# Head squares, gate scan, token sums and factors of a hybrid decoder layer in another order

## The reference

```python
xn = rmsnorm(x, norm_gain)
gb, gc, hc, zc, q, k, v, o, zm, ig, fg = split(xn @ w_in)        # nine of width 512, two of width 4
y_conv = gb * short_conv(gc * hc, conv_buf, conv_w) * silu(zc)   # 3 taps along the tokens
# mLSTM, 4 heads of 128, chunks of 128 tokens, one after another:
b = cumsum(log_sigmoid(fg)); log_d = causal(b[:, None] - b[None, :] + ig[None, :])
m_t = maximum(b + m_prev, max(log_d)); d = exp(log_d - m_t); inter = exp(b + m_prev - m_t)
s = (q @ k.T) * d
num = s @ v + inter * (q @ c_prev); den = sum(s) + inter * (q @ n_prev)
h = num / maximum(abs(den), exp(-m_t))
c_new = decay * c_prev + (w_last * k).T @ v                      # n_new likewise
h = h * rsqrt(mean(h * h) + EPS) * mh_norm_gain
y_m = h * sigmoid(o) * silu(zm)
out = rmsnorm(x + concat(y_conv, y_m) @ w_out, final_norm_gain)
```

## Time and profile before

| | |
|---|---|
| Median of 3 runs | 1103.79 us (1103.05 to 1104.08) |
| Profiled execution | 1105.74 us, its span 1103.7 us |
| TensorE matmul busy | 1027.2 us (93%) |
| TensorE weight load busy | 776.4 us (70%), beside the matmuls |
| DVE busy | 657.3 us (60%) |
| ACT busy | 423.4 us (38%) |
| POOL busy | 440.8 us (40%) |
| DMA | 180.86 MB, mean 164 GB/s |
| Chain that ended last | PE 61%, DVE 22%, ACT 5%, POOL 4%, issue 3%, DMA 3% |

### The profile page before, as it was taken

How to read it: one execution, slowest core, us unless ns; L and a number is a source line. 1 busy time by engine, 2 the same in 40 slices (tenths; PEclk the granted TensorE clock), 3 DMA queues, 4 the chain that set the end, 5 groups by cost and what they waited for, 6 DMA issues and landing times.

```text
span 1103.7 us, 22725 instructions
## 1 busy us (share of the span) xinstructions
PE 1027.2 (93%) x9052; PEld 776.4 (70%) x9052; DVE 657.3 (60%) x1156; ACT 423.4 (38%) x868; POOL 440.8 (40%) x477
## 2 busy tenths in 40 slices
PE   3799799999889988999999999999999999999995
PEld 2555545455478777999889899989889999444442
DVE  6786756664667776556775546567755544434343
ACT  6555443423334343334543443436343432211111
POOL 5211355445454484623542341427042330542422
PEclk9999899999889999999999999999999999999998
DMA  9686642924561256591605272943253659465651
GB/s 246 175 190 138 160 111 63 236 66 143 198 207 53 84 165 215 162 322 62 223 21 189 93 248 65 314 143 124 68 181 106 220 140 344 140 216 210 232 207 76
DMA packets 192077, 180.86 MB, mean 164 GB/s; under 512 B 44600, under 2 KB 152260, under 8 KB 191972
## 3 DMA queue, kind: packets, MB, share of 16 engines
q1 hardware_dynamic: 160880, 142.76, 41.8%
q0 software_dynamic: 7600, 25.03, 6.2%
q10 hardware_dynamic: 23492, 11.63, 3.6%
HBM read 120.48 MB, written 50.19 MB: 155 GB/s over the span
## 4 chain that ended last, share of the span: by engine, by line
PE 61%; DVE 22%; ACT 5%; POOL 4%; issue 3%; DMA 3%; SPq 1%; DVEq 0%; ACTq 0%; POOLq 0%
PE bank L1337 10%; PE bank L1339 10%; PE bank L1338 10%; PE bank L1562 4%; PE bank L1563 4%; PE bank L1561 4%; DVE xs L207 3%; DVE Wl L207 2%; DVE yc L207 2%; DVE gatebuf L207 2%; PE bank L1138 1%; PE bank L1140 1%; PE bank L1139 1%; PE bank L1494 1%; PE bank L1495 1%
## 5 line engine op out<-in xcount | busy, mean ns | idle before, releaser
L1337 PE MATMUL bank<-xTh,Wh 128*128 128x256 f16 x768 | 211.6, 275 | 12.8 <-ACT bank L207 8.1
L1338 PE MATMUL bank<-xTl,Wh 128*128 128x256 f16 x768 | 211.4, 275 | 0.0
L1339 PE MATMUL bank<-xTh,Wl 128*128 128x256 f16 x768 | 211.4, 275 | 0.0
L1138 PE MATMUL bank<-xTh,Wh 128*128 128x512 f16 (+2 forms) x440 | 122.8, 313 | 3.2 <-ACT tom L207 1.0
L1139 PE MATMUL bank<-xTl,Wh 128*128 128x512 f16 (+2 forms) x440 | 123.1, 312 | 0.0
L1140 PE MATMUL bank<-xTh,Wl 128*128 128x512 f16 (+2 forms) x440 | 123.1, 312 | 0.0
L1337 PEld LDWEIGHTS bank<-xTh,Wh 128*128 128x128 f16 x768 | 75.9, 99 | 25.8 <-ACT bank L207 6.9
L1338 PEld LDWEIGHTS bank<-xTl,Wh 128*128 128x128 f16 x768 | 75.9, 99 | 10.9 <-issue 0.7
L1339 PEld LDWEIGHTS bank<-xTh,Wl 128*128 128x128 f16 x768 | 75.9, 99 | 9.5
L1337 PE MATMUL bank<-xTh,xs 128*128 128x256 f16 x288 | 78.8, 274 | 2.0 <-DVE xs L207 2.0
L1339 PE MATMUL bank<-xTh,xs 128*128 128x256 f16 x288 | 78.9, 274 | 0.0
(11 more groups left out here) (529 smaller groups left out, 2857.1 us busy)
## 6 DMA issues: line engine op xcount, KB each, us to landing
xTh<-x_ops SPq DMA_DIRECT2D x12, 1280.0 KB, 8.9
xTl<-x_ops SPq DMA_DIRECT2D x12, 1280.0 KB, 12.2
wst<-in_w_in SPq DMA_DIRECT2D x25, 512.0 KB, 5.0
xs<-in_x_prompt SPq DMA_DIRECT2D x22, 512.0 KB, 4.0
y_ops<-ysumst POOLq DMA_DIRECT2D x16, 512.0 KB, 3.2
xTh<-x_ops SPq DMA_DIRECT2D x12, 512.0 KB, 5.0
xTl<-x_ops SPq DMA_DIRECT2D x12, 512.0 KB, 5.7
out<-xs POOLq DMA_DIRECT2D x11, 512.0 KB, 2.9
```

The source lines that it names most:

```text
L1138: mm(out, wh[:, k, :], xh, start=(k == 0), stop=False)
L1337: mm(out, wh[:, k, :], xh, start=(first and k == 0), stop=False, skip_group_check=not first)
L1338: mm(out, wh[:, k, :], xl, start=False, stop=False, skip_group_check=not first)
L1339: last = mm(out, wl[:, k, :], xh, start=False, stop=(k == KT // 2 - 1), skip_group_check=not first)
```

## The change

Normalisation of heads: all four squares stand behind ACT's seed of the first pair of the next block. `sel` is gone: its readers take the columns straight from `cols`, and a new semaphore `parts_ready` covers the exponents' operand. `den` comes in four instructions that read PSUM and `cols`, not five. `mhg` is scaled once at the start; the factor moves from the products `G` and `Gm` (and from `to`, `tom`) to `heads_out` and its sample counterpart. `factors` goes behind DVE's seed of the first pair.

Queues: gate scans of blocks 1 and 2 from GB to ZC, turns to O; x parts later on ACT and DVE (after `evacuate` and `at_end`); token sums spread in another way on POOL, ACT and DVE; for head 1 the weight splits in the order 0, 1 | 2, 3 (sums of pair 0) | 4 (V) | 5, 6, and SP loads ZC and O ahead of GB; `G` directly behind ZM's drain, with the mixed tile's products between. The diff, cut to its core (the indentation of the functions is taken off), first the constants:

```diff
-X_SQUARE = [{V: 6, Q: 7, GC: 8, HC: 9, ZC: 10, O: 11}, {K: 12, V: 13, Q: 14, HC: 15}, {K: 16}]
-X_PARTS = [{V: 5, Q: 6, GC: 7, HC: 8, ZC: 9, O: 10}, {K: 11, V: 12, Q: 13, HC: 14}, {K: 15, V: 16}]
+X_SQUARE = [{V: 6, Q: 7, GC: 8, HC: 9, ZC: 10, O: 11}, {K: 12, V: 13, Q: 14, O: 15}, {K: 16}]
+X_PARTS = [{V: 5, Q: 6, GC: 7, HC: 8, ZC: 9, O: 10}, {K: 11, V: 12, Q: 13, O: 14}, {K: 15, V: 16}]
...
-SCAN_AT = [O, GB, GB]
-TURN_AT = [ZM, ZC, ZC]
+SCAN_AT = [O, ZC, ZC]
+TURN_AT = [ZM, O, O]
...
-S_TAKE = [{}, {ZC: 0, ZM: 1}, {V: 2, HC: 3, ZM: 4}, {K: 5, Q: 6, HC: 7}]
-S_LOW = [{}, {ZC: 0, ZM: 1}, {V: 2, HC: 3, ZM: 4}, {K: 5, Q: 6, GB: 7}]
-S_STORE = [{}, {O: 0}, {K: 1, Q: 2, GB: 3}, {K: 4, V: 5, GC: 6, ZC: 7}]
+S_TAKE = [{}, {GC: 0, HC: 1}, {V: 2, GC: 3, ZC: 4, ZM: 5}, {Q: 6, HC: 7}]
+S_LOW = [{}, {HC: 0, GB: 1}, {Q: 2, HC: 3, ZM: 5}, {Q: 6, HC: 7}]
+S_STORE = [{}, {HC: 0, ZC: 1}, {Q: 2, GB: 3, O: 4}, {K: 5, GC: 6, ZC: 7}]
+S_LOW_NORMS = {2: 4}
...
-FIRST_SPLIT, HALF_SPLIT = [0, 3, 9, 11], [1, 4, 10, 12]
-V_SPLIT = 2
-T_SPLIT = [5, 7, 13, 15]
+FIRST_SPLIT = [[], [0, 5, 9, 11], [0, 3, 9, 11], [0, 3, 9, 11]]
+HALF_SPLIT = [[], [1, 6, 10, 12], [1, 4, 10, 12], [1, 4, 10, 12]]
+V_SPLIT = [None, 4, 2, 2]
```

SP, then POOL (`pool_block`, `pool_stream_block`), then TensorE (`at_end`):

```diff
-sp.wait_ge(op_low, splits(1, V_SPLIT))
-load_raw(1, GB)
-sp.wait_ge(op_low, splits(1, T_SPLIT[0] + 1))
+sp.wait_ge(op_low, splits(1, T_SPLIT[1][0] + 1))
 load_raw(1, ZC)
 load_raw(1, O)
+sp.wait_ge(op_low, splits(1, V_SPLIT[1]))
+load_raw(1, GB)
```

```diff
         y_operands(g, b - 1)
...
+        token_sums((0, 3, 7)[b - 1])
         store_sums(g, b - 1)
...
         if b == 2:
-            token_sums(3)
+            token_sums(4)
...
-        x_power(15)
-        token_sums(0)
+        token_sums(1)
     if b == NB - 1:
-        token_sums(7)
         weight_sums(1, 0)
     store_y(g, b, 0)
-    if b in (1, 2):
-        token_sums((1, 4)[b - 1])
+    if b == 2:
+        token_sums(5)
...
-    if b in (1, 2):
-        token_sums((2, 5)[b - 1])
+    if b == 1:
+        x_power(15)
+        token_sums(2)
...
-    for u in ((), (10,), (14,))[B] if B < 3 else ():
-        token_sums(u)
+    if B == 2:
+        token_sums(14)
     pool.wait_ge(t0_free, s_t0(nth(g, b), "hT") + 1)
     y_operands(*before)
     store_y(*before, 1)
-    if B == 2:
-        token_sums(15)
+    if B in (1, 2):
+        token_sums((10, 15)[B - 1])
...
     if B == 1:
+        pool.wait_ge(q_seed, pair_no(g, b, 2) + 1)
         token_sums(12)
```

```diff
-        pe.wait_ge(sel_ready, n + 1)
+        if b == 0:
+            pe.wait_ge(sel_ready, g + 1)
+        pe.wait_ge(parts_ready, b + 1)
```

ACT (`at_half`, `at_end`, `stream_block`, `act_block`):

```diff
-        if t in X_PARTS[b]:
-            x_high_part(X_PARTS[b][t])
-        if t in X_SQUARE[b]:
-            x_square(X_SQUARE[b][t])
+        if b == 0 and t == Q:
+            x_parts(b, V)
+        if b or t not in (V, Q):
+            x_parts(b, t)
...
-        act.wait_ge(sel_ready, n + 1)
...
     if first:
+        if b == 0 and t == Q:
+            x_parts(b, t)
         if t == GATES_AT[b]:
...
-        head_squares(n - 1, (2, 3))
+        head_squares(n - 1, range(CH))
...
-        token_sums_store(9)
-        token_sums_high(10)
...
+    if B == 1:
+        token_sums_store(9)
+        token_sums_high(10)
...
-    if B == 1:
-        token_sums_store(11)
-        token_sums_high(12)
...
+    if B == 1:
+        token_sums_store(11)
+        token_sums_high(12)
...
-    head_squares(n, (0, 1))
...
-            for i in {GC: (0, 1), GB: (2,), ZC: (3, 4), O: (5, 6)}.get(t, ()):
+            for i in {GC: (0, 1), ZC: (2, 3, 4, 5), O: (6,)}.get(t, ()):
```

DVE: gates, gate products, norms of the heads (`at_end` O, `head_norms`):

```diff
+    mark(tt(mparts[64:64 + H, block_of], rest, mparts[32:GR, block_of], ALU.subtract).then_inc(parts_ready, 1), parts_ready, b + 1)
...
-    mark(tt(dp[:, :], src[:, :], G[:, :], ALU.mult).then_inc(t0_free, 1), t0_free, at + 1)
+    mark(stt(dp[:, :], src[:, :], mhg[:, before:before + 1], G[:, :], ALU.mult, ALU.mult).then_inc(t0_free, 1), t0_free, at + 1)
...
-    mark(stt(cn[:, :], cn[:, :], sel[:, c, 2:3], kv[:, 0:DV1], ALU.mult, ALU.add).then_inc(free, 1), free, n * 3 + (2 + c // 2))
+    mark(stt(cn[:, :], cn[:, :], col(g, b, c, 2), kv[:, 0:DV1], ALU.mult, ALU.add).then_inc(free, 1), free, n * 3 + (2 + c // 2))
...
-        j, before = evacuations(g, b, O)
-        dve.wait_ge(p_free[j], before + 1)
-        did(ts(to[:, :], to[:, :], 1.0, mhg[:, bass.ds(g, 1)], ALU.add, ALU.mult))
...
+def gate_product(g, b):
...
+    j, before = evacuations(g, b, O)
+    dve.wait_ge(p_free[j], before + 1)
+    mark(stt(G[:, :], to[:, :], 1.0, zs[:, :], ALU.add, ALU.mult).then_inc(g_done, 1), g_done, n + 1)
...
-    mark(pick(sel[:, :, :], cols[:, 1 + CH * b:1 + CH * (b + 1), :, bass.ds(g, 1)].rearrange("p c k o -> p c (k o)"))
-         .then_inc(sel_ready, 1), sel_ready, n + 1)
...
+        head_norms(n)
+        if first and O in X_PARTS[b]:
+            x_low_part(X_PARTS[b][O])
+        if b in S_LOW_NORMS:
+            token_sums_low(S_LOW_NORMS[b])
+        if b == NB - 1:
+            split_low(1, 4)
+        head_means(n)
+        if first and O in X_SQUARE[b]:
+            x_gain(X_SQUARE[b][O])
+        if b == NB - 1:
+            split_low(1, 5)
+        head_scaled(n)
...
-        nv = N[i][:, 0:2 * DV1].rearrange("p (c v) -> p c v", c=2)
-        did(copy(den[:, 2 * i:2 * i + 2], nv[:, :, P]))
...
-    did(stt(den[:, :], den[:, :], -1.0, den[:, :], ALU.mult, ALU.max))
-    did(tt(den[:, :], den[:, :], sel[:, :, 0], ALU.max))
+        two = den[:, 2 * i:2 * i + 2]
+        sums = N[i][:, 0:2 * DV1].rearrange("p (c v) -> p c v", c=2)[:, :, P]
+        did(stt(two, sums, 1.0, col_of_chunks(g, b, 0, 2 * i, 2 * i + 2), ALU.mult, ALU.max))
+        did(stt(two, sums, -1.0, two, ALU.mult, ALU.max))
```

DVE: `stream_block` and `dve_block`:

```diff
-    if b == 0:
-        dve.wait_ge(prod, product_at(g, b, 0, M1))
-    if n == NB:
-        dve.wait_ge(dp_ready, n)
-    if b == 0:
-        factors(g)
     if B:
         head_means(n - 1)
-    mark(pick(sel[:, :, :], cols[:, 1 + CH * b:1 + CH * (b + 1), :, bass.ds(g, 1)].rearrange("p c k o -> p c (k o)"))
-         .then_inc(sel_ready, 1), sel_ready, n + 1)
     seed(g, b, 0)
     if B:
         head_scaled(n - 1)
+    if b == 0:
+        factors(g)
...
-    if B == 1:
-        token_sums_low(9)
...
-        token_sums_low(10)
+        token_sums_low(9)
...
+    if B == 1:
+        token_sums_low(10)
...
-    if B == 1:
-        token_sums_low(11)
...
-        token_sums_low(12)
+        token_sums_low(11)
...
+    if B == 1:
+        token_sums_low(12)
...
-    did(ts(to[:, :], to[:, :], 1.0, mhg[:, bass.ds(g, 1)], ALU.add, ALU.mult))
-    mark(stt(G[:, :], to[:, :], 0.25 / WS, zs[:, :], ALU.mult, ALU.mult).then_inc(g_done, 1), g_done, n + 1)
+    mark(stt(G[:, :], to[:, :], 1.0, zs[:, :], ALU.add, ALU.mult).then_inc(g_done, 1), g_done, n + 1)
...
-        if b == 0:
+        if b == 0 and t != ZM:
             mixed_start(g, b, t, first)
         at_half(g, b, t, first)
         if first:
             gate_chain(b, t)
+            if b == 0 and t == Q:
+                x_parts(b, V)
         if b == 0 and t == HC:
             mixed_conv(g)
             did(copy(u[:, 0:2], um[:, META:META + 2]))
         evacuate(g, b, t)
-        if first:
-            if t in X_PARTS[b]:
-                x_low_part(X_PARTS[b][t])
-            if t in X_SQUARE[b]:
-                x_gain(X_SQUARE[b][t])
+        if t == ZM:
+            if b == 0:
+                mixed_start(g, b, t, first)
+            gate_product(g, b)
         at_end(g, b, t, first)
+        if first and t != O and (b or t != V):
+            x_parts(b, t)
         if t in S_LOW[b]:
             token_sums_low(S_LOW[b][t])
         if b == NB - 1:
             if t == GC:
                 split_low(1, 0)
                 split_low(1, 1)
-            if t == GB:
+            if t == ZC:
                 split_low(1, 2)
-            if t == ZC:
                 split_low(1, 3)
-                split_low(1, 4)
-            if t == O:
-                split_low(1, 5)
+            if t == ZM:
                 split_low(1, 6)
```

More of the change, by code:

```diff
@@ L1771, in at_end @@
                             cc = slice(c * P, (c + 1) * P)
-                            last = fn(out[:, cc], src[:, cc], ACT.Exp, bias=sel[:, c, kind:kind + 1])
+                            last = fn(out[:, cc], src[:, cc], ACT.Exp, bias=col(g, b, c, kind))
                             if c < CH - 1:
@@ L1836, in split_high @@
             def split_high(g, i):
-                src, (high, _) = split_operand(i)
-                if i in T_SPLIT or i - 1 in T_SPLIT:
-                    p = T_SPLIT.index(i if i in T_SPLIT else i - 1)
+                first, half, sums = FIRST_SPLIT[g], HALF_SPLIT[g], T_SPLIT[g]
+                src, (high, _) = split_operand(g, i)
+                if i in sums or i - 1 in sums:
+                    p = sums.index(i if i in sums else i - 1)
                     act.wait_ge(op_sums, 16 * (g - 1) + 4 * p + 4)
                 else:
```

(21 more changed lines are left out.)

111 lines of the change are left out of this document (54 added, 57 removed).

## The result

| | before | changed |
|---|---|---|
| Median | 1103.93 us (1103.05 to 1104.26, 4 runs) | 1097.24 us (1095.66 to 1098.38, 4 runs) |
| Ratio | | 0.9933, interval 0.9912 to 0.9954 |
| Profiled execution | 1105.74, span 1103.7 | 1095.66, span 1093.7 |
| PE / DVE / ACT / POOL busy | 1027.2 / 657.3 / 423.4 / 440.8 | 1022.5 / 652.6 / 422.3 / 428.2 |

Faster by 6.7 us in the medians and by 10.1 us between the two profiled executions (10.0 in their spans); forecast were 35.3. A second set of runs of the changed kernel gave a ratio of 0.9931 (0.9915 to 0.9946).

What follows compares the result with a forecast made beforehand. TensorE's matmuls bound the last 471 us; earlier, waits mostly on DVE and ACT, and half clock after long ones, cost time. Gains 20.5 + 9.0 + 10.8 = 40.3, less 5 reserve, 35.3: 1068.5 us, range 1056 to 1090.

Steps and rivals of the forecast that it cites:

- V and columns: Head 0, blocks 1 and 2: earlier ZM drain and state round remove waits, 4.1 and 5.9 us won with the clock.
- the first pair: Start of the stream: reordered splits and ZM's drain remove waits of 2.0 and 2.7 us with half clock, 9.0 us won.
- moves from ahead of DVE's seed to behind the scaled heads: Starts of heads 2 and 3: moving `factors` removes waits for DVE's seed of 1.8 and 1.4 us, 3.2 us won.
- Following its order I get a wait of some 3.4 us: Head 0, gate logits before the third state round: DVE now bounds, wait 2.1 us longer plus 1.5 us half clock.
- DVE stays the bound of blocks 0 to 2: Rival, head 0: DVE's work there hardly shrinks, so 14.3 us and half the reserve are affected; some 1080 us, chance 0.25.
- I take 1.0, since the same seed now also stands behind high part 10: Block 1 of head 1: y operands ahead of token sums 10 remove a 1.4 us ACT seed wait; 1.0 us won.
- the scan's own waits: Head 0, blocks 1 and 2: the moved gate scan delays chunk products by 1.4 and 0.9 us; 2.3 given back, bounds 0 and 5.
- The term of the seed at 377.58: Second stream block's start: the 2.24 us seed wait goes; after 1.2 us or less of new wait, 2.8 us remain won.
- In block 0 the number: Head 0: `qfm` wait goes but x unit 8's transpose holds block 1's logits, 1.0 us won; `tom` wait adds 1.0.
- The fifth's copy: Rival, stream block starts: behind four squares, the fifth product's copy comes late at all 11 boundaries; about 1114 us, chance 0.05.
- The reserve of 5 us: Whole kernel: 5 us held back from the 40.3 us sum for new waits in places not followed instruction by instruction.
- it does not do what it says: Rival, whole kernel: order written out but other waits hold each stage; -8 us or less, 1096, chance 0.05 (little effect).

Runs made afterwards that it cites:

- head0_x_behind_round: Changed kernel; head 0: token sums 0, 1 at old tiles, ACT's tile Q x parts behind exponentials, DVE's (block 1) behind third state round: 1086.17 us, ratio 0.9826.
- late_and_mixed_sums: Changed kernel with `factors` behind `heads_out`; in head 1's block 1, high and low part 10 later, low part 11 and store of sums 11 earlier: 1080.90 us, ratio 0.9778.
- mended_scan_at_gb: all_three_mended with the gate scans of blocks 1 and 2 back at GB, in front of the first update of `cn`: 1068.35 us, ratio 0.9658 to the kernel before.
- all_three_mended: Changed kernel with the edits of late_and_mixed_sums and head0_x_behind_round together: 1069.15 us, ratio 0.9668 to the kernel before.

## Why the prediction was wrong, by its own steps

The sign and most of the removals were right. The ledger above has them within 0.7 us at seven places: V and columns, the scan, `sel`, `dp`, ZC of block 3, the first pair, low part 9. "What is late next" was wrong, at four places.

1. *`factors` "moves from ahead of DVE's seed to behind the scaled heads", and two waits go.* They do (+3.8), and waits of 3.9 and 4.0 us come in their place, with the clock at 0.79 in the 8 us behind the first (520.9 to 528.9) and 0.62 around the second (727 to 736): -11.8, and -1.5 at head 1. The step charged nothing for the six at their new place, where they take 5.5 us and not 1.5, and did not look at what GpSimd does there. The same text had the row for it. It also told the rule of the Trainium skill short: SBUF — State Buffer, "Who interferes with whom", exempts a DVE instruction with one SBUF input only outside the two-port modes, and lists copy, cast and tensor_scalar among those that can enter them, if their operands fit. By that the six can contend. The trace agrees: `selm`, one input of 80x2, took 1.24 us beside the sums and 0.17 without. This was the largest error, some 12 us.

2. *"Following its order I get a wait of some 3.4 us... 3.6 us given back; bounds 0 and 6."* 9.9 were given back, outside the bounds: 4.9 us wait at the logits, 2.5 and 1.1 ahead of it. The step has no term for GpSimd or ACT in this stretch. Token sums 0 had moved into it and stretched a product from 1.23 to 2.96 us; ACT's x part then stood between that product and the exponentials; and DVE's own x part stood ahead of the third round. head0_x_behind_round, with all three out of the way, is 11.6 us faster than the changed kernel. The rival "DVE stays the bound of blocks 0 to 2" named part of this and priced it at the 14.3 us of these blocks less half the reserve, 1080; it alone was not enough, for by the ledger the blocks were some 9.4 us short of their 14.3.

3. *The load of block 2's x sums* has no term. The store of sums 11 moved behind two tanhs on ACT, SP's load waits for that store, and TensorE for the load: 3.4 us, ledger -4.9. With the store earlier the wait is gone (late_and_mixed_sums). But the load also landed after 8.7 us there and 10.7 here, and no run has the one without the other: how much is the store and how much the transfer stays open.

4. *"I take 1.0, since the same seed now also stands behind high part 10."* -1.5: GpSimd's sums 10, now behind the y operands, ended at 377.84, the high part at 378.9, the seed only then; the wait was 3.0 and not 0.4. The sign was wrong because the high part's own wait for these sums was left out.

Smaller: the scan's own waits cost 4.9 and not 2.3, and by mended_scan_at_gb the move was worth nothing once the rest was in order. The term of the seed at 377.58 had the right sum (2.8) by luck, with the wrong cause: the order of the squares does nothing in either kernel, and that the new `den` and the removed scalings did it together is argued, not shown. In block 0 the number was near (1.2 for 2.0) by luck too: a lead of 5.7 us at 56 was gone by 84, to waits for the mixed tile's own DVE work (the longest 1.86 at 80.46), before unit 8 could hold anything. In nine of the runs unit 8 did hold the logits, for 1.2 to 2.2 us. The fifth's copy never set a block start: at the only one with a wait for DVE's seed (1.0 us, at 361.94) it was done 1.6 us before that seed began. The waits of 3.9 us at heads 2 and 3 stand at the V tile, where the list of what would show it had nothing.

The reserve of 5 us for places not followed was the wrong kind: such places held some 18 us (11.8, 1.5 and 4.9), and a fixed list of each move past a queue might have found them. The time was nearest to the rival "it does not do what it says" (1096), but by another mechanism; all_three_mended at 1069.15 lies beside the forecast of 1068.5, but it has other edits in it (`factors` further back, x parts and sums elsewhere); it shows what the new waits cost, 29 us, and does not bear out the forecast's terms.

## What to carry to other kernels

When an instruction is moved, look up what the engine that shares its memory access does at the new place, and take the duration from there: the shortest DVE instructions were stretched the most here (0.17 to 1.24 us). When two engines hold the same chain side by side, mending one can show nothing; try both before either is called harmless. For each move write down the whole relay (sum, high part, low part, store, load, use) and not only the engine on which it happens.
